# Hybrid encoder block with 64 routed experts: experts with one block of tokens and with several taken alternately, and the last three items added by one-hot products

## The reference, cut to what matters

```python
scores = sigmoid(xf @ w_router)                 # 64 experts, top 8 of 4 groups
w = take(scores, eidx); w = w / sum(w) * 2.5
# assignments sorted by expert, each expert's rows padded to blocks of 128
h = silu(xb @ w_gate[e]) * (xb @ w_up[e])       # 128x1024 by 1024x256, twice
out = (h @ w_down[e]) * gate[:, None]           # 128x256 by 256x1024
y = y.at[tok].add(out)
```

## Time and profile before

| | |
|---|---|
| device time, median of 3 runs | 1412.65 us (1407.62 to 1412.69) |
| device time of the profiled execution | 1411.65 us |
| its span | 1410.0 us |
| TensorE busy | 1309.5 us, 93% |
| VectorE, ScalarE, GpSimd busy | 875.7, 738.1, 459.0 us |
| first product to router | 0 to about 354 us |
| shared expert, tables | about 354 to 448 us |
| 93 items | 453.4 (first SiLU) to 1350.8 us (last) |
| after the last SiLU | 59.2 us |

### The profile page before, as it was taken

How to read it: one execution, slowest core, us unless ns; L and a number is a source line. 1 busy time by engine, 2 the same in 40 slices (tenths; PEclk the granted TensorE clock), 3 DMA queues, 4 the chain that set the end, 5 groups by cost and what they waited for, 6 DMA issues and landing times.

```text
span 1410.0 us, 25859 instructions
## 1 busy us (share of the span) xinstructions
PE 1309.5 (93%) x5960; PEld 1024.4 (73%) x5962; DVE 875.7 (62%) x1318; ACT 738.1 (52%) x1044; POOL 459.0 (33%) x608
## 2 busy tenths in 40 slices
PE   6899988999999999999989999999999999999960
PEld 5785466888444887888878888788877788888850
DVE  4430444345665676767866567776687666775846
ACT  4421244211011676767865657766677666775822
POOL 1431201000001344434443344334343434443435
PEclk9999999999999999999999999999999999999985
DMA  9464032002306799999999889999899989999987
GB/s 336 150 180 160 0 119 90 40 36 80 152 5 241 248 302 340 327 305 326 339 365 280 259 250 318 363 344 282 253 366 376 325 249 306 325 339 278 295 257 279
DMA packets 99535, 348.47 MB, mean 247 GB/s; under 512 B 13104, under 2 KB 33584, under 8 KB 82736
## 3 DMA queue, kind: packets, MB, share of 16 engines
q1 hardware_dynamic: 72144, 263.64, 48.7%
q0 software_dynamic: 27360, 84.44, 26.4%
HBM read 294.85 MB, written 71.57 MB: 260 GB/s over the span
## 4 chain that ended last, share of the span: by engine, by line
PE 71%; DMA 14%; ACT 3%; issue 3%; DVE 2%; POOL 1%; DVEq 1%; ACTq 1%; SPq 0%; POOLq 0%
PE ps L721 26%; PE ps_out L735 13%; DMA raw_gu<-in_w_up 8%; PE ps L613 6%; PE ps L481 5%; PE ps L464 5%; DMA raw_dn<-in_w_down 5%; PE ps L648 4%; PE ps L515 4%; PE ps L564 2%; ACT w_gu L919 1%; DMA y_rows_dram<-ob,idxs 1%; PE ps_out L630 1%; PE ps L743 1%; PE ps L658 1%
## 5 line engine op out<-in xcount | busy, mean ns | idle before, releaser
L721 PE MATMUL ps<-w_gu,xTh 128*128 x1504 | 477.9, 399 | 13.2 <-DVE xTl L1297 11.1
L1144 DVE TENSOR_TENSOR w_gu<-raw_gu,w_gu (+1 forms) x256 | 302.6, 1223 | 63.8 <-ACT w_gu L919 62.9
L721 PEld LDWEIGHTS ps<-w_gu,xTh 128*128 128x128 f32 x1504 | 279.0, 190 | 73.5 <-issue 19.3
L721 PE MATMUL ps<-w_gu,xTl 128*128 x752 | 296.6, 394 | 0.0
L919 ACT ACTIVATE w_gu<-raw_gu (+1 forms) x256 | 256.8, 1060 | 23.7 <-SPq L387 23.7
L735 PE MATMUL ps_out<-w_dn,hTh 128*128 x744 | 242.1, 407 | 0.0
L1492 POOL DMA_INDIRECT y_rows_dram<-ob,idxs x93 | 151.7, 1632 | 194.8 <-ACT ob L940 175.9
L1151 DVE TENSOR_TENSOR w_dn<-raw_dn,w_dn (+1 forms) x128 | 150.9, 1221 | 84.0 <-ACT w_dn L923 83.6
L721 PEld LDWEIGHTS ps<-w_gu,xTl 128*128 128x128 f32 x752 | 142.6, 190 | 30.0
L735 PEld LDWEIGHTS ps_out<-w_dn,hTh 128*128 128x128 f32 x744 | 133.1, 189 | 25.1
L735 PE MATMUL ps_out<-w_dn,hTl 128*128 x372 | 145.9, 392 | 0.0
(11 more groups left out here) (206 smaller groups left out, 1554.8 us busy)
## 6 DMA issues: line engine op xcount, KB each, us to landing
raw_gu<-in_w_gate SPq DMA_DIRECT2D x64, 1024.0 KB, 7.5
raw_gu<-in_w_up SPq DMA_DIRECT2D x64, 1024.0 KB, 10.8
raw_dn<-in_w_down SPq DMA_DIRECT2D x64, 1024.0 KB, 14.8
y_rows_dram<-zero SPq DMA_DIRECT2D x1, 9216.0 KB, 37.6
x_ring<-in_x SPq DMA_DIRECT2D x8, 512.0 KB, 5.0
w_in_sb<-in_w_in SPq DMA_DIRECT2D x8, 512.0 KB, 9.7
xh<-in_x SPq DMA_DIRECT2D x8, 512.0 KB, 8.2
w_out_sb<-in_w_out SPq DMA_DIRECT2D x1, 4096.0 KB, 12.9
```

Source lines behind the costliest of these rows:

```text
L721: mm = pe.matmul(ps[3][:, :], x_[:, k, :], w_gu[:, bass.ds(at, 1), part, :, k, :], start=(k == 0 and part == 0 and x_ is xTh), stop=(k == ...
L1144: dv.tensor_tensor(gu_part(w_gu[:, :, 1, :, :, :], at, m), gu_part(raw_gu, at, m), gu_part(w_gu[:, :, 0, :, :, :], at, m).bitcast(F32), AL ...
```

## The change: what it does

Routing also makes an order of the experts: single and double ones get keys by their rank among their kind, so that they alternate evenly (`key_t`, `upto`), and a third row of `tab` says which expert is at a place in the order. With the counts above the blocks per place are 1 2 1 2 1 2 ..., with two singles next to each other in six places, and a single one first and last. SyncE loads in this order, so the first loads wait for `tab`. The gate and up weights are split in 2 parts of 2048 columns. Tables 0 to 5 are summed one shared product later than before, tables 6 and 7 after two of the down products. On VectorE and ScalarE the look into the table stands behind `gated_h` and `silu`. The last turn is written out: no item 93 is computed, items 90 to 92 are not scattered; their results are split by value and added by products with one-hot matrices that GpSimd makes (`last_rows`, 96 matmuls). There are two copies of the rows in DRAM in place of three; the second is added into the first by accumulating DMAs into SBUF. At the start, chunks 3 and 4 of x are loaded ahead of small tables, and chunk 1 is normalised and turned later.

```diff
-GU_PARTS = 4
+GU_PARTS = 2
...
-            v = t[:, bass.ds(at, 1), m // 2, (m % 2) * 4:(m % 2) * 4 + 4, :]
-            return v.rearrange("p a k f -> p (a k) f")
+            return t[:, bass.ds(at, 1), m, :, :].rearrange("p a k f -> p (a k) f")
...
+            sp.dma_start(lng_row[:, :], spread(ln_g, DA)).then_inc(s_small, 16)
+            sp.dma_start(lnb_row[:, :], spread(ln_b, DA)).then_inc(s_small, 16)
+            next_x(3)
...
+            next_x(4)
...
-            for e in range(2):
-                load_gu(sp, e, 1 - e)
-                load_dn(sp, e, 1 - e)
...
+            sp.wait_ge(s_tab, 1)
+            for j in range(2):
+                e = look(sp, 2, j, NE - 1)
+                load_gu(sp, e, 1 - j)
+                load_dn(sp, e, 1 - j)
...
+            def load_next_gu(j, at):
+                sp.wait_ge(s_hg, (j - 1) * GU_PARTS)
                 sp.sem_inc(s_turn_sp, 1)
-                sp.wait_ge(s_lg, (e - 1) * GU_PARTS)
+                sp.wait_ge(s_lg, (j - 1) * GU_PARTS)
                 sp.sem_inc(s_turn_sp, 1)
...
-            last = last_item(sp)
-            sp.wait_ge(s_gu, last + 1)
-            sp.sem_inc(s_turn_sp, 1)
-            for c in range(NC // 2, NC):
-                sp.dma_start(yb_in[1][:, c - NC // 2, :], yv2[c]).then_inc(s_x[c], 16)
-            n = turns(sp)
-            for u in range(TURN):
-                sp.wait_ge(s_add[u], n * 16)
-                sp.sem_inc(s_turn_sp, 1)
-            for c in range(NC):
-                sp.dma_start(yc_in[:, c, :], yv3[c]).then_inc(s_yl[c], 16)
             for c in range(NC):
...
+                        if k == 4:
+                            turn_x(1)
...
-                if c + 1 < NC:
+                if 1 <= c < NC - 1:
...
+            pe.wait_ge(s_kinds, 1)
+            pe.matmul(ps[6][:, 0:NE], multi[:, :], tri[0:NE, 0:NE], start=True, stop=True)
+            pe.matmul(ps[6][:, NE:2 * NE], multi[:, :], identb[:, :], start=True, stop=True)
+            pe.matmul(ps[6][:, 2 * NE:2 * NE + 1], multi[:, :], ones[0:NE, 0:1], start=True, stop=True).then_inc(s_pm, 1)
+            s_gate_up(1, 0)
...
+            pe.matmul(ps[7][:, 0:NE], nchb[:, :], upto[:, :], start=True, stop=True)
+            pe.matmul(ps[7][:, NE:2 * NE], nchb[:, :], identb[:, :], start=True, stop=True)
+            pe.matmul(ps[7][:, 2 * NE:3 * NE], ones[0:NE, :], upto[:, :], start=True, stop=True)
+            pe.matmul(ps[7][:, 3 * NE:3 * NE + 1], nchb[:, :], ones[0:NE, 0:1], start=True, stop=True).then_inc(s_pm, 1)
+            s_gate_up(1, 1)
...
+            pe.matmul(ps[6][0:3, 0:P], cols[:, 0:3], ident[:, :], start=True, stop=True).then_inc(s_pm, 1)
             s_gate_up(2, 0)
+            s_gate_up(2, 1)
             table(0)
             table(1)
-            s_gate_up(2, 1)
+            s_gate_up(3, 0)
             table(2)
             table(3)
-            s_gate_up(3, 0)
+            s_gate_up(3, 1)
             table(4)
             table(5)
-            s_gate_up(3, 1)
-            table(6)
-            table(7)
...
+            def last_rows(c, items):
+                banks = ((0, 1), (2, 3), (4, 5))[c % 3]
+                for half, bank in enumerate(banks):
+                    for u in items:
+                        for part, ob_ in enumerate((ob_high[:, u, :], ob_rest[u])):
+                            mm = pe.matmul(ps[bank][:, :], onehot[:, u, c * P:(c + 1) * P],
+                                           ob_[:, half * 512:(half + 1) * 512], start=(u == 0 and part == 0),
+                                           stop=(u == TURN - 1 and part == 1))
+                if TURN - 1 in items:
+                    mm.then_inc(s_lastmm, 1)
...
+            s_down(0)
+            s_down(1)
+            table(6)
+            table(7)
+            for c in range(2, 6):
                 s_down(c)
...
+            two_less = turns_less(pe, 4, 2)
+            turn_of_items(two_less + 1, expert(two_less * TURN + (TURN - 1)), final=True)
             down(last, *expert(last))
+            pe.wait_ge(s_oh, TURN)
+            pe.wait_ge(s_obh, TURN - 1)
+            pe.wait_ge(s_obl, TURN - 1)
+            for c in range(3):
+                last_rows(c, range(TURN - 1))
+            pe.wait_ge(s_obh, TURN)
+            pe.wait_ge(s_obl, TURN)
+            for c in range(3):
+                last_rows(c, (TURN - 1,))
+            for c in range(3, NC):
+                pe.wait_ge(s_sum, c - 2)
+                last_rows(c, range(TURN))
...
                 ahead = expert(i + 2)
-                silu(i)
                 evac_xT(i + 1)
+                if isinstance(i, int) and i == 0:
+                    act.wait_ge(s_yst[0], 16 * 4)
 
                 with act.If(ahead[0] > 0):
                     act.wait_ge(s_rg, ahead[1] + 1)
-                    split_gu(ahead[2], (0, 1))
+                    split_gu(ahead[2], (0,))
                 evac_h(i)
                 if not (isinstance(i, int) and i == 0):
                     evac_out(i - 1, (u - 1) % TURN, turn if u else turn - 1)
                 with act.If(ahead[0] > 0):
-                    split_gu(ahead[2], (2, 3))
+                    split_gu(ahead[2], (1,))
...
+            act.wait_ge(s_oa, last)
+            for u in range(TURN - 1):
+                act.activation(ob_high[:, u, :], ob[:, u, :], ACT.Copy).then_inc(s_obh, 1)
+            act.wait_ge(s_dn, last + 1)
+            act.activation(ob_high[:, TURN - 1, :], ps_out[:, :], ACT.Copy).then_inc(s_obh, 1)
...
             norm_x(0)
-            norm_x(1)
             for c in range(NC):
                 evac_x(c)
                 rest_x(c)
                 if c == 0:
 
                     for k in range(KD):
+                        if k == 2:
+                            norm_x(1)
...
+            step(dv.tensor_scalar(multi[:, :], ps[5][0:NE, 0:1].to_broadcast([NE, P]), float(P), None, ALU.is_gt))
+            dv.sem_inc(s_kinds, 1)
...
+            dv.wait_ge(s_pm, 2)
+            before, is_multi = ps[6][0:NE, 0:NE], ps[6][0:NE, NE:2 * NE]
+            n_multi, n_single = kinds[:, 0:1], kinds[:, 1:2]
+            many((dv.tensor_scalar(n_multi, ps[6][0:NE, 2 * NE:2 * NE + 1], 1.0, None, ALU.max),
+                  dv.tensor_scalar(kinds[:, 2:3], ps[6][0:NE, 2 * NE:2 * NE + 1], -1.0, float(NE), ALU.mult, ALU.add),
+                  dv.tensor_tensor(key_t[:, 0, :], count_row[0:NE, 0:NE], before, ALU.subtract)))
+            step(dv.tensor_scalar(n_single, kinds[:, 2:3], 1.0, None, ALU.max))
+            many((dv.tensor_scalar(key_t[:, 0, :], key_t[:, 0, :], 0.5, n_multi, ALU.add, ALU.mult),
+                  dv.tensor_scalar(key_t[:, 1, :], before, 0.5, n_single, ALU.add, ALU.mult)))
+            step(dv.scalar_tensor_tensor(out=key_t[:, 1, :], in0=key_t[:, 1, :], scalar=0.25, in1=key_t[:, 0, :],
+                                         op0=ALU.add, op1=ALU.subtract))
+            step(dv.tensor_tensor(key_t[:, 1, :], key_t[:, 1, :], is_multi, ALU.mult))
+            step(dv.tensor_tensor(key_t[:, 0, :], key_t[:, 0, :], key_t[:, 1, :], ALU.add))
+            step(dv.tensor_tensor(key_t[:, 2, :], key_t[:, 0, :], ident[0:NE, 0:NE], ALU.mult))
+            step(dv.tensor_reduce(kinds[:, 3:4], key_t[:, 2, :], AX.X, ALU.add))
+            step(dv.tensor_scalar(upto[:, :], key_t[:, 0, :], kinds[:, 3:4], None, ALU.is_ge))
+            dv.sem_inc(s_chunks, 1)
...
+            shared_h(3)
...
+                gated_h(i, u)
...
                 ahead = expert(i + 2)
-                gated_h(i, u)
                 rest_xT(i + 1)
+                if isinstance(i, int) and i == 0:
+                    dv.wait_ge(s_yst[1], 16 * 4)
                 with dv.If(ahead[0] > 0):
-                    rest_gu(ahead[2], ahead[1], (0, 1))
+                    rest_gu(ahead[2], ahead[1], (0,))
                 rest_h(i)
                 with dv.If(ahead[0] > 0):
-                    rest_gu(ahead[2], ahead[1], (2, 3))
+                    rest_gu(ahead[2], ahead[1], (1,))
...
+            for u in range(TURN - 1):
+                dv.wait_ge(s_obh, u + 1)
+                dv.tensor_tensor(ob_rest[u][:, :], ob[:, u, :], ob_high[:, u, :].bitcast(F32), ALU.subtract).then_inc(s_obl, 1)
+            dv.wait_ge(s_obh, TURN)
+            dv.tensor_tensor(ob_rest[TURN - 1][:, :], ps_out[:, :], ob_high[:, TURN - 1, :].bitcast(F32),
+                             ALU.subtract).then_inc(s_obl, 1)
+
...
+            def add_last(c):
                 dv.wait_ge(s_yl[c], 16)
-                dv.tensor_tensor(ya_in[:, c, :], ya_in[:, c, :], yc_in[:, c, :], ALU.add).then_inc(s_sum, 1)
...
+                dv.wait_ge(s_lastmm, c + 1)
+                for half, bank in enumerate(((0, 1), (2, 3), (4, 5))[c % 3]):
+                    piece = ya_in[:, c, half * 512:(half + 1) * 512]
+                    ins = dv.tensor_tensor(piece, ps[bank][:, :], piece, ALU.add)
+                ins.then_inc(s_sum, 1)
...
+            two_less = turns_less(gp, 4, 2)
```

(37 more changed lines are left out.)

178 lines of the change are left out of this document (93 added, 85 removed).

## The result

The changed kernel takes 1433.65 us (median of 4 runs, 1431.54 to 1436.14), the kernel before in the same session 1412.67 (4 runs, 1407.62 to 1414.3). The ratio is 1.0151, 95% interval 1.0126 to 1.0176: slower by 21 us. Forecast was 1403, range 1380 to 1417, with a chance of 0.11 for slower.

What follows compares the result with a forecast made beforehand. TensorE, busy 93% of the span, was taken as the bound, so only its stalls and the end could be won. Start -6.3, tables +10.6, first item +2.9, loop +1.6, end -17.2 gave -8.4: 1403.2 us, range 1380 to 1417.

Steps and rivals of the forecast that it cites:

- Loop: Items between the SiLUs: alternation removes DMA-bound runs, each single costs 1.1 us; stalls 34 us, +1.6 in sum.
- late signals from SyncE, whose release moves back with the rest, and the debt of DMA I put at 2: In the loop: SyncE's later signals and DMA's debt were together to cost 2 us.
- The price of the wide part: In the loop, VectorE waits for ScalarE's wider splits: 0.8 us more per item of this kind, 1.1 for a single.
- Rival (a): In the loop, the wider part costs nothing on the path, 0.3 a single; loop -22, time 1380; chance 0.22.
- That alternation pays: In the loop, alternating singles and doubles ends DMA as a bound: 26.8 us a pair, under TensorE's 28.1.
- Routing and tables: Before and among the first down products: moved tables stall TensorE, with a slow restart; +10.6 us, bounds +4 and +14.
- Rival (b): At the tables: their move does not stall, the middle costs 2 in place of 10.6; time 1394; chance 0.14.
- Start: Loading chunk 3 of x first removes ScalarE's wait and TensorE's gap; -6.3 us, bounds 0 and -8.
- First item: Between SiLU 0 and 1: VectorE does two rest passes before gated_h(0); +2.9 us, bounds -2 and +5.
- End: From last SiLU to end: 42 us in place of 59.2, paced by last_rows and accumulating DMAs; -17.2, bounds -10 and -20.
- Rival (c): At the end: accumulating loads one after the other at 8.93 us set the end; time 1449, slower; chance 0.08.

Runs made afterwards that it cites:

- e12: The changed kernel with SyncE's table look moved ahead of its waits for the free raw buffers; 1412.5 us, ratio 1.0005.
- e5: The changed kernel with SyncE giving the landed signal before it waits for the next load's buffer, not after; 1412.5 us, ratio 1.0013.
- e6: The changed kernel with gate/up weights in four parts and SyncE's landed signals given first; 1394.8 us, ratio 0.9896.
- e10: The kernel before with one edit, gate/up weights split in two parts of 2048 columns; 1409.9 us, ratio 0.9993.
- e1: The changed kernel with gate/up weights split in four parts of 1024 columns again; 1397.9 us, ratio 0.9906.
- e13: The changed kernel with experts in order of their numbers and SyncE's load numbers from the loop counter, no table look; 1411.9 us, ratio 1.0004.
- e9: The changed kernel with four parts and experts in order of their numbers; 1405.7 us, ratio 0.9973.
- the best version: The changed kernel with four parts, landed signals first, tables at their old places and one-hots on VectorE; 1382.6 us, ratio 0.9809.
- e14: The best version with SyncE's table look moved ahead of the waits too; 1391.0 us, ratio 0.986 against the kernel before.
- e8: The changed kernel with the three one-hot operations on VectorE in place of GpSimd; 1434.0 us, ratio 1.0167.

## Why the prediction was wrong

*Loop: wrong, and this decides.* The step that failed is "late signals from SyncE, whose release moves back with the rest, and the debt of DMA I put at 2". About 20 us stand in its place. I had counted as lateness the rest that frees the raw buffer, some tenths of a microsecond. I left out what the diff adds between this release and the signal, the look on SyncE, though it stands in the diff behind the very wait that I wrote of. It is 1.28 us (1.86 against 0.58) at each single. It moves ScalarE's first split back by 0.5 us (3.09 against 2.56), and a single by as much (1.77 against 1.28). The 29 singles behind a double make 14 of the 20 us. The five behind a single, which cost 0.9 each in the changed kernel (I had 0.2) and 0.1 in e12, make another 4. Moving the look takes away 20.1 us of stalls (e12), and giving the signal ahead of it and of the load as much (e5: 20.6). With the other parts as they came and the forecast's loop the time would have been 1412, inside the range.

*The price of the wide part: nearly right.* Without the delay of the look the loop has 35.6 us of stalls; the forecast was 34, with 1.1 for a single, and 1.2 to 1.3 were measured. That the sums agree so well is in part luck: 29 times 1.2 are 35, where I had 31, and the 3 us that I added for neighbouring singles, late signals and DMA were hardly needed. The wide rest took 2.29 us, as the Trainium skill's formula ("VectorE: DVE Perf Modes", TRN2 errata) had it. Singles follow each other in five places, not six (35 singles and 29 doubles; five intervals of 10.2 to 10.6 mark them in the changed kernel): 29 times 1.1 and 5 times 0.2 would have made the loop 1 us longer. With the signals first, four parts instead of two take away 19.4 (e5 to e6). Rival (a), that the width is free, fell for this kernel. In the kernel before it holds for the sum alone (e10): a single behind a double costs 0.8 there, with 10.2 for the item, and why other items give it back was not tested. With four narrow parts the late signal costs only 3.6 (e1 to e6): the two costs stand in one chain and are not additive.

*That alternation pays: right only where DMA was the bound.* The runs of 11.4 us are gone. But with wide parts little is left of it even with the look out of the way: stalls of 40.3 us without and 35.6 with alternation (e13, e12), and the dearer first item eats that (1411.9 against 1412.5 us). With narrow parts it pays 8 to 10 us (e9 to e1).

*Routing and tables: right, a little small.* From the last tables to `s_down` 8.2 us (forecast 7.9), 2.9 for the slow restart (2.5), 2.7 for the third product (2.1). The 0.5 us of the small matmuls stands in the text of the forecast and not in its +10.6, and its start adds up to -6.5, not -6.3. Rival (b) fell. *Start: right at its place, 1.4 short behind it.* The chain of the changed kernel has the third chunk's products without a gap:

```profile
41.79 10.93 PE ps L485 x48
```

The earlier trace rows had 45.49 and 13.77: 6.5 us gained at its end. At the last tables of the shared expert only 5.25 are left (411.40 against 416.65 in the earlier trace rows), where the forecast had 6.65; what took 1.4 between was not tried. Together +7.1 instead of +4.3.

*First item: right.* 13.3 us, forecast about 14; other runs of the same order had 13.0 to 16.3. VectorE waits for the stored rows as worked out, then has the rests to do:

```profile
460.08 4.50 DVE L1206 TENSOR_TENSOR w_gu<-raw_gu,w_gu  x2 [1.50 <-DMA y_rows_dram<-xh]
```

*End: mechanism right, size off by 5.5.* Rival (c), accumulating transfers one after the other at 8.9 us, fell. Timelines of VectorE and GpSimd, to set against the earlier trace rows:

```profile
1388.52 3.32 DVE L1447 TENSOR_TENSOR ob_rest<-ob,ob_high 128x1024 fp32r<-128x1024 f32 x2 [1.58 <-ACT ob_high L1051]
...
1400.11 1.29 DVE L1458 TENSOR_TENSOR ya_in<-ps,ya_in 128x512 f32<-128x512 f32 x2 [7.03 <-DMA ya_in<-y_rows_dram]
...
1410.06 1.29 DVE L1458 TENSOR_TENSOR ya_in<-ps,ya_in 128x512 f32<-128x512 f32 x2
...
1420.68 1.29 DVE L1458 TENSOR_TENSOR ya_in<-ps,ya_in 128x512 f32<-128x512 f32 x2 [1.34 <-DMA ya_in<-y_rows_dram]
...
1425.12 1.28 DVE L1468 SCALAR_TENSOR_TENSOR ya_in<-ya_in,rs,gf_row 128x1024 f32<-128x1024 f32 x1 [0.77 <-POOL rs L1508]
```

```profile
1382.81 8.55 POOL L1634 TENSOR_SCALAR onehot<-tok_row,slot_col 128x1024 fp32r<-128x1024 f16 x3 [6.88 <-DVE w_dn L1213]
1391.29 6.37 POOL L1642 DMA_DIRECT2D ya_in<-y_rows_dram  x7
```

The last seven of the eight chunks follow the first in 20.6 us, 2.9 each, where 3.0 were charged. But they are not even: up to the fifth (1410.06) they come 2.5 us apart, and the last three, beside which the stores run from 1407.62 on, take 10.6 us together, 3.5 each. My working had no stores in this stretch; at 2.5 each the last add would come 3.1 us sooner. That the stores are the reason is read from the times and not tested. So the last add begins 37.6 us behind the last SiLU where I had 32 to 33, and from there to the end are 9.9 us where I had 9.

## What to carry to other kernels

When a change adds an operation to an engine that only waits, issues and signals, put it on that engine's timeline between each wait and each signal, since a signal in program order waits for everything ahead of it. Here 1.3 us of lookup on SyncE cost 21 us of time beside the wide parts, and moving it ahead of the wait gave them back. Beside narrow parts the late signal cost 3.6 us of stalls, and in the best version the move lost 8 us (e14). A cost found by undoing one part of a change (four parts instead of two: 36 us) need not belong to that part; put the part alone into the kernel before as well. Where two engines hand work to each other in a chain that is just full, as here, a delay that finds no slack left is paid once for each repetition: 0.5 us of a late split, some 30 times.

## What the runs showed of the hardware

- TensorE restarted slowly after 7.09 us of idle time. The granted clock of the changed kernel around the first `s_down`, busy times as in the windows above:

```profile
419.60:426.20 6.60, 6.60 (x9) 2.87 (x10) 0.00 (x0) 0.00 (x0) 0.00 (x0) 0.56 0.01 2
426.20:430.00 3.80, 3.80 (x18) 1.80 (x17) 0.00 (x0) 0.00 (x0) 0.00 (x0) 1.00 0.00 0
```

  After 7.09 us without work the granted clock is 0.56, near the lower level, 1.2 GHz, and eight products take 6.57 us; the next eight have 2.4 GHz (1.00) and take 3.60. So a stall of 7.1 us cost 10.
- An operation of one input and 1024 columns, f16 to fp32r, took 2.85 us on GpSimd and 0.69 on VectorE (e8).
- The first two `ob_rest` took 3.32 us of VectorE together while GpSimd made its third one-hot, and 2.36 in e8, where GpSimd made none. By the Trainium skill ("SBUF — State Buffer", the section on who interferes with whom) a Vector instruction with both inputs in SBUF contends with a GpSimd instruction that reads SBUF; these rows agree. The third `ob_rest`, which reads one input from PSUM, took 1.22 and 1.23, but it began after the last one-hot had ended and so tests nothing.
- Accumulating transfers from HBM into SBUF held the DMA engines full at 202 to 221 GB/s, 2.5 us for each 512 KB, half the rate of the plain loads ahead of them (397 to 422).
